# Layer norm by column halves and quarters, an early split of the router's weights, and a first gather of two experts

## What is computed

```python
def _layer_norm(x, g, b):
    xf = x.astype(jnp.float32)
    mu = jnp.mean(xf, axis=-1, keepdims=True)
    var = jnp.mean(jnp.square(xf - mu), axis=-1, keepdims=True)
    return ((xf - mu) * lax.rsqrt(var + LN_EPS) * g + b).astype(x.dtype)
...
x = _layer_norm(DN_ALPHA * x + 0.5 * _swiglu(x, ffn1_w1[l], ffn1_w2[l]), ln1_g[l], ln1_b[l])
```

```python
g_w, g_idx = lax.top_k(jax.nn.softmax(g_logits, axis=-1), 1)
...
e_w, e_idx = lax.top_k(jax.nn.softmax(e_logits, axis=-1), MOE_TOP_K)
...
h = jax.nn.silu(xb @ w_gate[e]) * (xb @ w_up[e])
return h @ w_down[e]
```

## Time and profile before

| | us |
|---|---|
| median of 3 runs | 2864.51 (2863.2 to 2865.44) |
| profiled execution | 2863.64 |
| its span | 2861.6 |
| TensorE products busy | 2665.7 (93%) |
| TensorE weight loads busy | 1958.4 (68%) |
| VectorE busy | 1282.7 (45%) |
| ScalarE busy | 1029.2 (36%) |
| GpSimd busy | 69.0 (2%) |
| mean granted TensorE clock | 0.984 |

### The profile page before, as it was taken

The page is one execution under the profiler, slowest core; times in us unless marked ns, Lnnn a source line. Parts: engine busy times, 40 slices in busy tenths (PEclk is TensorE's granted clock), DMA queues, the critical chain, the costliest instruction groups (busy, mean ns, idle before and its releaser), DMA issues.

```text
span 2861.6 us, 40274 instructions
## 1 busy us (share of the span) xinstructions
PE 2665.7 (93%) x16540; PEld 1958.4 (68%) x16540; DVE 1282.7 (45%) x2346; ACT 1029.2 (36%) x1629; POOL 69.0 (2%) x28
## 2 busy tenths in 40 slices
PE   8999999999999999999989989989988999998996
PEld 7988888899898988889888744333336864333333
DVE  5565554755656565565678641111116653111112
ACT  4444563444444465344457531111114442111111
POOL 0001000100100100010010000000000000000000
PEclk9999999999999999999999999999999999999999
DMA  9636643565463843456353379999996219999996
GB/s 307 214 111 160 211 100 127 172 206 177 162 206 102 243 144 92 162 167 201 119 164 119 100 272 422 421 421 422 421 417 202 89 49 421 421 422 421 421 421 290
DMA packets 313986, 695.32 MB, mean 243 GB/s; under 512 B 57104, under 2 KB 242320, under 8 KB 264656
## 3 DMA queue, kind: packets, MB, share of 16 engines
q1 hardware_dynamic: 310896, 682.24, 65.1%
q10 hardware_dynamic: 2912, 10.52, 1.2%
HBM read 691.63 MB, written 1.08 MB: 242 GB/s over the span
## 4 chain that ended last, share of the span: by engine, by line
PE 62%; DMA 21%; DVE 10%; ACT 5%; issue 2%; SPq 0%; ACTq 0%; DVEq 0%
PE ps L282 25%; DMA ring<-in_moe_w_gate 20%; PE ps L790 7%; PE ps L2518 7%; PE ps L1533 3%; PE ps L1573 3%; DVE weight_parts L223 3%; PE ps L313 3%; PE ps L2535 2%; PE ps L2568 2%; PE ps L294 2%; ACT weight_parts L215 1%; PE ps L2456 1%; PE ps L1460 1%; DVE tiny L906 1%
## 5 line engine op out<-in xcount | busy, mean ns | idle before, releaser
L282 PE MATMUL ps<-xT_upper,weight_parts 128*128 128x256 f32 (+1 forms) x4656 | 851.8, 285 | 25.1 <-DVE xT_lower L932 11.3
L223 DVE TENSOR_TENSOR weight_parts<-ring,weight_parts 128x1024 fp32r<-128x1024 f32 x479 | 612.3, 1281 | 502.1 <-ACT weight_parts L215 501.7
L282 PEld LDWEIGHTS ps<-xT_upper,weight_parts 128*128 128x128 f32 (+1 forms) x4656 | 722.4, 190 | 50.2 <-issue 19.4
L215 ACT ACTIVATE weight_parts<-ring 128x1024 fp32r<-128x1024 f32 x479 | 503.9, 1055 | 544.2 <-PE ps L282 326.3
L282 PE MATMUL ps<-xT_lower,weight_parts 128*128 128x256 f32 (+1 forms) x2328 | 658.1, 283 | 0.0
L282 PEld LDWEIGHTS ps<-xT_lower,weight_parts 128*128 128x128 f32 (+1 forms) x2328 | 441.4, 190 | 0.2
L2518 PE MATMUL ps<-ring,bias_tiles 128*64 128x512 f32 x1024 | 240.2, 596 | 33.7 <-DMA ring<-in_moe_w_gate 17.9
L2518 PE MATMUL ps<-ring,arena 128*64 128x512 f32 x1024 | 240.4, 596 | 33.0 <-DMA ring<-in_moe_w_gate 17.2
L2807 DVE TENSOR_TENSOR bias_tiles<-ps,bias_tiles 128x512 f32<-128x512 f32 x32 | 22.1, 692 | 503.5 <-ACT bias_tiles L2664 503.5
L2568 PE MATMUL ps<-moe_slots,bias_tiles 128*64 128x512 f32 x1024 | 229.2, 596 | 4.4 <-ACT bias_tiles L2667 4.4
L790 PE MATMUL ps<-weight_parts,hidden_upper 128*128 128x512 f32 x704 | 218.4, 391 | 1.7 <-DVE hidden_lower L842 1.7
(11 more groups left out here) (325 smaller groups left out, 2847.9 us busy)
## 6 DMA issues: line engine op xcount, KB each, us to landing
ring<-in_ffn_w SPq DMA_DIRECT2D x132, 1024.0 KB, 5.2
ring<-in_moe_w_up SPq DMA_DIRECT2D x128, 1024.0 KB, 24.3
ring<-in_moe_w_gate SPq DMA_DIRECT2D x128, 1024.0 KB, 24.4
moe_slots<-in_moe_w_down SPq DMA_DIRECT2D x128, 1024.0 KB, 20.2
ring<-in_w_gate SPq DMA_DIRECT2D x24, 1024.0 KB, 7.6
ring<-in_w_in SPq DMA_DIRECT2D x20, 1024.0 KB, 7.2
ring<-in_ssd_w_in SPq DMA_DIRECT2D x20, 1024.0 KB, 5.4
ring<-in_attn_w_qkv SPq DMA_DIRECT2D x18, 1024.0 KB, 9.6
```

The lines of the kernel that those rows point to most:

```text
L215: act.activation(self.part(n, 0), cut(self.stream.slot(pos)), ACT.Copy).then_inc(self.upper_done, 1)
L223: dve.tensor_tensor(self.part(n, 1), cut(self.stream.slot(pos)), self.part(n, 0).bitcast(F32), ALU.subtract).then_inc(self.split, 1)
L282: m = pe.matmul(out[0:rows, :], w[of_w][:, k, :], c.xTp[of_x][:, k, :], start=(k == 0 and (of_w, of_x) == PARTS[0]), stop=(k == KT - 1 and ...
```

## The change

- Each stage ahead of a norm ends in quarters (row tile by column half), and each quarter is signalled (`LAST_PARTS`, `parts_done`). In a feed-forward stage a quarter takes the products of both halves of the last hidden columns.
- The norm sums and takes statistics by quarters. The epsilon is the root's bias now. ScalarE normalises the first tile in two halves and the first half of the second; VectorE does the last quarter itself. TensorE turns four column tiles as soon as their half is there. ScalarE makes the upper part of the first tile's second half before that of the second tile's first. In the last norm VectorE does all of it by halves, and a store is a quarter.
- The clock-keeping block between the tiles is 512 columns in place of 1024, and the one ahead of the router's products is gone.
- The router's weights are loaded to a place of their own, for the first expert layer in the setup, for the second in the first expert stage, and split in the norm. Their ring slot is gone.
- In the expert stage GpSimd makes the lower row part of the second tile, some small operations are joined or moved, the first turn gathers for two experts (128 slots), the transposes of the slots (`turned`) move into the first turn behind the hidden products, and the other two experts' gather follows them.

```diff
-ARENA = 14192
...
-CLOCK_ROWS, CLOCK_PARTS, CLOCK_ROUTER = (512, 1024), 1024, (1024, 2560, 512, 512)
+ARENA = 13888
+CLOCK_ROWS, CLOCK_PARTS, CLOCK_ROUTER = (512, 512), 1024, (1024, 2560, 512, 512)
...
-def row_products(c, pe, n, parts, k, t, ends):
+LAST_PARTS = ((0, 0), (0, 1), (1, 0), (1, 1))
+def parts_done(c, last):
+    return [[(c.acc.sem, c.acc.at(1)), (c.acc.sem, c.acc.at(2))], [(c.acc.sem, c.acc.at(3)), (c.units.done, last + 1)]]
+def row_products(c, pe, n, parts, k, t, ends, halves=(0, 1)):
...
                     for half in range(2):
                         for t in range(TT):
                             down(n, half, t)
-            down(CHUNKS - 1, 0, 0)
-            down(CHUNKS - 1, 1, 0).then_inc(c.acc.sem, c.acc.one())
-            down(CHUNKS - 1, 0, 1)
-            down(CHUNKS - 1, 1, 1)
+            for t, side in LAST_PARTS:
+                for half in range(2):
+                    mm = down(CHUNKS - 1, half, t, (side,))
+                if (t, side) != LAST_PARTS[-1]:
+                    mm.then_inc(c.acc.sem, c.acc.one())
...
-        def sums(t):
-            dve.wait_ge(*done[t])
-            ch.link(dve, dve.scalar_tensor_tensor(c.x[:, t, :], c.x[:, t, :], ALPHA / weight,
-                                                  ps[:, 2 * t:2 * t + 2, :].rearrange("p b n -> p (b n)"),
-                                                  ALU.mult, ALU.add))
-        def variance(t):
-            for h in range(2):
-                ins = dve.bn_stats(stats[:, t, h, :], c.x[:, t, h * 512:(h + 1) * 512])
-            ch.link(dve, ins)
-            ch.link(dve, dve.bn_aggr(mv[:, t, :], stats[:, t, :, :].rearrange("p h n -> p (h n)")))
-            dve.tensor_scalar(st[:, t, 0:1], mv[:, t, 1:2], LN_EPS / weight ** 2, None, ALU.add).then_inc(c.stat.sem, c.stat.one())
+        def side(t, h):
+            return c.x[:, t, h * 512:(h + 1) * 512]
+        def sums(t, h):
+            dve.wait_ge(*done[t][h])
+            ch.link(dve, dve.scalar_tensor_tensor(side(t, h), side(t, h), ALPHA / weight, ps[:, 2 * t + h, :], ALU.mult, ALU.add))
+            ins = dve.bn_stats(stats[:, t, h, :], side(t, h))
+            if h == 1:
+                ch.link(dve, ins)
+                dve.bn_aggr(mv[:, t, :], stats[:, t, :, :].rearrange("p h n -> p (h n)")).then_inc(c.stat.sem, c.stat.one())
...
+        def finished(t):
+            dve.wait_ge(c.stat.sem, c.stat.at(t + 1))
+            for h in range(2):
+                ins = dve.scalar_tensor_tensor(side(t, h), side(t, h), mv[:, t, 0:1], c.norm[:, 0, h * 512:(h + 1) * 512], ALU.subtract, ALU.mult)
+            dve.wait_ge(c.std.sem, c.std.at(t + 1))
+            ch.link(dve, ins)
+            ch.link(dve, dve.reciprocal(st[:, t, 2:3], st[:, t, 1:2]))
+            for h in range(2):
+                dve.scalar_tensor_tensor(side(t, h), side(t, h), st[:, t, 2:3], c.norm[:, 1, h * 512:(h + 1) * 512],
+                                         ALU.mult, ALU.add).then_inc(c.mix.sem, c.mix.one())
...
-            dve.wait_ge(c.xT_hi.sem, c.xT_hi.at(n + 1))
+            dve.wait_ge(c.xT_hi.sem, c.xT_hi.at((0, 2, 1, 3)[n] + 1))
...
-        sums(0)
-        variance(0)
-        scales(0)
-        sums(1)
-        variance(1)
-        scales(1)
         if last:
+            dve.wait_ge(c.norm_loaded.sem, c.norm_loaded.issued)
             for t in range(TT):
-                dve.wait_ge(c.x_new.sem, c.x_new.at(t + 1))
-                if t == 0:
-                    dve.wait_ge(c.norm_loaded.sem, c.norm_loaded.issued)
-                ch.link(dve, dve.tensor_tensor(c.x[:, t, :], c.x[:, t, :], c.norm[:, 0, :], ALU.mult))
-                dve.tensor_tensor(c.x[:, t, :], c.x[:, t, :], c.norm[:, 1, :], ALU.add).then_inc(c.mix.sem, c.mix.one())
+                for h in range(2):
+                    sums(t, h)
+                finished(t)
         else:
+            sums(0, 0)
+            sums(0, 1)
+            sums(1, 0)
+            scales(0)
+            sums(1, 1)
+            scales(1)
+            dve.tensor_scalar(side(1, 1), side(1, 1), mv[:, 1, 0:1], st[:, 1, 2:3], ALU.subtract, ALU.mult).then_inc(c.x_last.sem, c.x_last.one())
             raw(0)
             for n in lead[0:1]:
                 c.units.lower(dve, n)
+            if router:
+                dve.wait_ge(R.hi.sem, R.hi.at(1))
+                dve.tensor_tensor(c.router_parts[1], c.router_w[:, :], c.router_parts[0].bitcast(F32), ALU.subtract).then_inc(R.split.sem, R.split.one())
             raw(1)
             for n in range(4):
...
+        def normed(t, halves=(0, 1)):
             act.wait_ge(c.rstd.sem, c.rstd.at(t + 1))
-            act.activation(c.x[:, t, :], c.x[:, t, :], ACT.Identity, scale=st[:, t, 2:3], bias=st[:, t, 3:4]
-                           ).then_inc(c.x_new.sem, c.x_new.one())
+            for h in halves:
+                v = c.x[:, t, h * 512:(h + 1) * 512]
+                act.activation(v, v, ACT.Identity, scale=st[:, t, 2:3], bias=st[:, t, 3:4]).then_inc(c.x_new.sem, c.x_new.one())
...
+            normed(0)
             for n in lead[0:1]:
                 c.units.upper(act, n)
-        normed(1)
+            if router:
+                act.wait_ge(c.units.done, c.units.limit)
+                act.wait_ge(R.landed.sem, R.landed.issued)
+                act.activation(c.router_parts[0], c.router_w[:, :], ACT.Copy).then_inc(R.hi.sem, R.hi.one())
+        deviation(1)
         if not last:
+            normed(1, (0,))
             raw(0)
             upper(0)
+            upper(2)
             upper(1)
-            upper(2)
             raw(1)
             upper(3)
...
             for t in range(TT):
                 keep_clock(c, pe, CLOCK_ROWS[t])
-                pe.wait_ge(c.x_new.sem, c.x_new.at(t + 1))
                 for k in range(KT):
+                    if k % 4 == 0:
+                        ready = c.x_last.at(1) if t and k else c.x_new.at(2 * t + k // 4 + 1)
+                        pe.wait_ge((c.x_last if t and k else c.x_new).sem, ready)
                     m = pe.transpose(ps[:, 4 + 2 * t + k // 4, (k % 4) * P:(k % 4 + 1) * P],
                                      c.x[:, t, k * P:(k + 1) * P], c.ident[:, :])
                     if k % 4 == 3:
                         m.then_inc(c.xT_ps.sem, c.xT_ps.one())
...
-        c.stored.issued += 32
+        c.stored.issued += 64
...
                 for k in (6, 7):
-                    m = row_products(c, pe, plan.out[k], m_parts, k, t, 7)
-                    if t == 1:
+                    m = row_products(c, pe, plan.out[k], m_parts, k, t, 7, (half,))
+                    if (t, half) == LAST_PARTS[-1]:
                         m.then_inc(c.units.done, 1)
-                if t == 0:
+                if (t, half) != LAST_PARTS[-1]:
                     m.then_inc(c.acc.sem, c.acc.one())
...
                 pe.wait_ge(K.chosen, m + 1)
-                if m == 0:
+                if m == 0 and cols.start == 0:
                     pe.wait_ge(c.x_split.sem, c.x_split.at(2))
+                    pe.wait_ge(c.aux_dve.sem, c.aux_dve.at(4))
+                elif m == 0:
+                    pe.wait_ge(K.xe, half + 1)
                 else:
-                    pe.wait_ge(K.xe, 2 * m + half)
+                    pe.wait_ge(K.xe, 2 * m + half + 2)
                 o = gathered_banks(m, half).rearrange("p b (k n) -> p (b k) n", k=2)
                 for k in range(4):
                     f = (4 * half + k) * P
                     for t in range(TT):
                         for part in range(2):
-                            mm = pe.matmul(o[:, k, :], x_parts[part][:, t, f:f + P], chosen[:, t, :],
+                            mm = pe.matmul(o[:, k, cols], x_parts[part][:, t, f:f + P], chosen[:, t, cols],
                                            start=(t == 0 and part == 0), stop=(t == 1 and part == 1))
                 mm.then_inc(K.gathered, 1)
-            keep_clock(c, pe, CLOCK_ROUTER[0], 0)
-            pe.wait_ge(R.split.sem, R.split.at(1))
+            pe.wait_ge(R.split.sem, R.split.at(0))
             for k in range(KT):
                 if k % 4 == 0:
                     pe.wait_ge(c.x_parts.sem, c.x_parts.at(k // 4 - 1))
...
+            pe.wait_ge(c.aux_dve.sem, c.aux_dve.at(1))
             for t in range(TT):
-                for u in range(TT):
+                for u in range(t + 1):
                     m = pe.matmul(ps[:, COUNTS, t * 64:t * 64 + 32], c.tri[:, u, t * P:(t + 1) * P], mask[:, u, :],
...
+            gather(0, 0, TURN_COLS[0])
             pe.wait_ge(c.aux_dve.sem, c.aux_dve.at(5))
             pe.transpose(ps[0:1, MOST, 0:P], most[:, 0:1], c.ident[:, :]).then_inc(c.aux_pe.sem, c.aux_pe.one())
-            keep_clock(c, pe, CLOCK_ROUTER[3])
-            gather(0, 0)
...
-            for t in range(TT):
-                pe.transpose(ps[0:64, TURNED, t * P:(t + 1) * P], slots[:, t, :, :].rearrange("p r n -> p (r n)"), c.ident[:, :])
```

(57 more changed lines are left out.)

## The result

| | before | changed |
|---|---|---|
| median, us | 2864.38 (6 runs, 2862.87 to 2865.8) | 2875.79 (6 runs, 2874.04 to 2877.26) |
| ratio | | 1.0041, 95% interval 1.0031 to 1.0052 |
| span of the profiled execution | 2861.6 | 2873.1 |

What follows compares the result with a forecast made beforehand. TensorE held 62% of the span, weight transfers 21%, with the expert stages ending by their transfers. Terms +0.6 - 1.1 - 3.3 - 1.5 - 1.2 - 1.5 = -8.0 us gave a median of 2856.5, range 2852 to 2866.

Steps and rivals of the forecast that it cites:

- The first expert stage, forecast -3.3: Norm, router and first expert stage: first turn starts 4.3 us earlier, its down products come 1.0 later after that, together -3.3.
- I take 4 and nothing on the path: Router ahead of the first expert stage: GpSimd's lower row part takes 4 us, covered until the token choice.
- 0.95 for the lower clock, as before: First gather: 0.95 us added for the lower clock, on top of 3.85 us for its 32 narrow products.
- The price of a narrow product: Two-expert gather: a 128-column product takes 0.12 us, so 32 take 3.85 us and narrowing wins nothing.
- Rivals 1: Gathers: narrow products cost the plain 0.213 us each, in all -2.0 us, 2862.5; chance 0.30.
- 2 (0.06): Gathers: weight loads are hidden, a narrow product takes 0.06 us, in all -11.0 us, 2853.5; chance 0.08.
- The second expert stage, forecast -1.2 - 1.5: Second expert stage: input and transfers 1.2 us earlier; last norm behind it: taken as 1.5 us shorter.
- its longer first turn is hidden by ten pieces: Second expert stage: ten pieces still to load, some 25 us of transfers, hide the longer first turn.
- The ordinary norms: Six norms: each gains 0.55 us, but four behind feed-forward stages pay +0.7; together +0.6 and, behind two mixers, -1.1.
- the root begins 0.5 earlier: Ordinary norms: the second root begins 0.5 us earlier, not 1.5, as ScalarE isn't free before.
- Norm 8, forecast -1.5: Norm behind the first expert stage: half the 1024-column block goes, -1.0 us, and the conversion order gives -0.5.
- Rival 3: Norms: less clock-keeping work drops TensorE to 1.2 GHz, 2.6 us a norm in seven, +18.2, 2874.7; chance 0.08.

Runs made afterwards that it cites:

- e2: The changed kernel with 96 unused words in front of the weight parts outside the expert stages: 2867.97 us, ratio 1.0016.
- e3: The changed kernel with the second tile's lower row part back on VectorE, behind the first choice: 2874.03 us, ratio 1.0036.
- e14: e10 with the lower part of the second tile's rows on GpSimd again: 2861.52 us, ratio 0.9996.
- e5: The changed kernel with 4,608 clock-keeping columns in place of 2,560 behind the router's products: 2876.81 us, ratio 1.0047.
- e6: The changed kernel with the first gather making all four experts' 256 columns and no second gather in the first turn: 2870.46 us, ratio 1.0027.
- e10: e9 with the 24 first-gather products that need no lower part of the second tile made first, then the other 8: 2858.73 us, ratio 0.9982.
- e7: The changed kernel with the edits of e2, e3, e5 and e6 and 1,024 filler columns between a norm's row tiles: 2862.36 us, ratio 0.9995.
- e9: e7 with the transposes of the slots ahead of the first turn again: 2857.16 us, ratio 0.9977.
- e13: e10 with the change's narrow first gather of two experts, the other two experts' in the turn: 2857.32 us, ratio 0.9977.
- e8: The kernel before with 24 unused words in front of the weight parts outside the expert stages: 2867.21 us, ratio 1.0017.
- e4: The changed kernel with a feed-forward stage's last hidden columns multiplied in the old order for the first row tile: 2875.46 us, ratio 1.0044.

## Why the prediction was wrong, step by step

The forecast was -8.0 us, measured are +11.5 in the profile: 19.5 apart. "Slower" had been given a chance of 0.09.

- **A term that the forecast didn't have: the place of the tiles, 7.2 us by the ratios of the changed kernel and e2, 8.4 by their profiles up to norm 7.** The forecast went through instructions, waits and queues, and took every untouched product at its old price, without a reason. The new tile was in the diff, and no step looked at it. It is most of the 11.5 us; without it some 4 are left, still slower and not faster.
- **The first expert stage, forecast -3.3, measured +2.2: 5.5 us.** The input did come earlier, and that the second turn's down weights set the stage was right (issued 2.0 us later from E, the stage 2.2 longer). The forecast's terms for that issue failed: the gather was to begin 23.8 us from E, and began at 25.4; from there to the first turn it was 7.1 us, not 5.4; from the turn's start to its down products 23.0, not 21.0. Two steps lie behind this. (1) "I take 4 and nothing on the path" for GpSimd's row part: it took 2.85, less than assumed, but held VectorE for it, and only the wait for GpSimd's result was priced, not what it does to VectorE. The kernel before showed it, in a row that I hadn't read. GpSimd, then VectorE beside it, before:

```profile
236.78 11.42 POOL L1030 TENSOR_TENSOR x_rows<-x_rows,norm_params 128x1024 f32<-128x1024 f32 x4 [236.33 <-DVE weight_parts L223]
```

```profile
236.88 6.71 DVE L223 TENSOR_TENSOR weight_parts<-ring,weight_parts 128x1024 fp32r<-128x1024 f32 x2
...
243.76 2.19 DVE L1345 TENSOR_TENSOR arena<-arena 128x8 f32<-128x8 f32 x2
```

  Two operations that take 1.22 us each lasted 6.71, two of 128x8 2.19. The Trainium skill states a rule for this, on the page SBUF — State Buffer, section SBUF: two separate sides: VectorE and GpSimd share one pair of ports, and where VectorE has two SBUF inputs and GpSimd reads SBUF, one of them holds it for a whole instruction while the other waits. The traces agree: 2.77 us with GpSimd's operation beside it, 0.23 without (e3), 2.82 with it again (e14). (2) "0.95 for the lower clock, as before": the clock was low over the whole gather and 4 us more. TensorE had rested 5.4 us ahead of it, but a rest of 2.0 was enough too (e5); wide products behind the same rest had the clock back within the gather (e6), and with the rest nearly filled and no stop by GpSimd it didn't fall (e10). The moved transposes of the slots were no failed step: with the second gather they took 4.0 us, 4.3 were forecast. They had a price that this gather covered, VectorE's steps behind them, 1.6 us on the gating (e7, e9).
- **The price of a narrow product, right.** 0.12 was taken; at full clock 32 took 3.61 us, 0.113 each, and 16 wide ones 2.11, 0.132 each (changed kernel):

```profile
1713.05 3.77 PE L2519 MATMUL ps<-moe_rounded 128*128 128x128 f32 x32
1716.66 0.71 PE L2609 MATMUL ps<-ident,bias_tiles 128*128 128x128 f32 x4
...
1717.73 2.18 PE L2519 MATMUL ps<-moe_rounded 128*128 128x256 f32 x16
```

  Rivals 1 (0.213) and 2 (0.06) fall. The sign against the forecast, 16 narrow products in 3.4 us or more, did show in the first gather (3.68), but by the low clock, 0.22 each. The 81 ns of the Trainium skill's page TensorE: Matmul & The Clock Gate, section Back-to-back issue gap, would have made these 32 products 2.6 us (an estimate from that page); the row says 3.61.
- **The second expert stage, forecast -1.2 - 1.5, measured +0.35: 3.0 us.** Its transfers began 1.5 us earlier from E, and from the last scatter products to the end it took 1.2 less: both near the forecast (1.2 and 1.5). Wrong was "its longer first turn is hidden by ten pieces". The second turn's down weights were issued 50.3 us behind the first transfer, 46.9 before, and the queue ran dry (2415 to 2421). A row that shows transfers at full rate says nothing of how much slack there is. The issue came 3.4 us later and the gap is worth 2.6 us of transfers at 421 GB/s, so the slack was under 1 us (an estimate). e10 issues them after 42.5, and the gap is gone.
- **The ordinary norms, forecast +0.15 behind a feed-forward stage, -0.55 behind a mixer.** Behind the former: -0.39 to the first product, -0.4 to -0.5 in the first chunk, +0.68 in the last: about -0.2. Behind the latter the first product came 0.78 and 0.50 later, and 0.4 came back in the chunk: VectorE's last weight part was still ahead of the first quarter, and the scales behind the third, so ScalarE began later, not earlier. With the 0.55 a norm that was forecast as a gain, the forecast is off by some 1.6 us in these two. That "the root begins 0.5 earlier" was for one kind 1.0, for the other -0.2.
- **Norm 8, forecast -1.5, measured -1.56 to the first product (8.35 us).** Right, and with the filler of 1,024 columns back it is 8.79 to 10.08 (e7, e9, e10, e13, e14), so that block has the part the forecast gave it.
- **Rival 3** gave 2874.7 for a fall of the clock in seven norms, at 2.6 us each. The time is near, the mechanism was a small part of it. The clock did fall behind norms 3, 4 and 6 (at 728, 929 and 1431 us), where it had not before; behind norm 3 that cost 1.1 us of the first chunk (13.21 us, behind norm 2 12.07). e3, e5 and e6 have the same three falls. e2, with the same filler of 512 columns and only the tiles moved, has none there, and its stages behind these norms are 2.7, 2.5 and 1.6 us shorter, of which the chunks explain 1.6 in the first; e10, with 1,024 columns, has one behind norm 4. So neither the filler nor the place alone is shown to set them. They also differ between executions of one kernel: the twelve of e8 took 2863.90 to 2865.55 us at a mean clock of 0.986 to 0.988, and 2868.86 to 2874.79 at 0.983 or 0.984. Some 3 to 4 us of the 19.5 are what is left when the points above are summed, with 1.4 given back by the feed-forward norms; these falls are where I look for them, and that wasn't tried.

## What to carry to other kernels

A tile that is added or resized moves all tiles behind it, and that can change the price of every product: compare a long steady stretch of an untouched loop first, before any wait is explained, and keep a few idle words to move tiles with. Before work goes to an idle engine, look in the trace for what the others do while that engine works. Where a stage ends by its transfers, price an edit by when it frees the slots, turn by turn, and measure the slack; a full rate alone isn't slack.

## What the runs showed of the hardware

- The 256-column products of the feed-forward stages took 0.1183 or 0.1200 us each by the first byte of their weight tiles modulo 256 (160 against 0 and 32), at the same granted clock, 1.4% of such a product and 0.25% of the kernel.
- A GpSimd operation of 2.85 us that reads and writes SBUF stretched a VectorE operation with two SBUF inputs from 0.23 to between 2.75 and 2.82 us, in both expert stages of six kernels (changed, e2, e4, e5, e6, e14).
- Behind a rest of 5.4 us and 2 us of filler, the clock stayed at 1.2 GHz through 32 products with 128 columns (both expert stages of the changed kernel, 7.1 us each), and was at 2.4 GHz 0.9 and 3.2 us into those with 256 columns (e6). In e3 and e5, with other rests, it stayed low through the narrow products too. In e13 it was high when 32 narrow products began, and fell 2.6 us into them; in e10, at the same place with wide ones, it stayed.
